# Both turns of a pair of 64 column heads ahead of values and scores in one step

## The reference

```
s = jnp.einsum('bhqd,bhld->bhql', qi, ko) * scale     # scores, masked
p = jax.nn.softmax(s, axis=-1)
o = jnp.einsum('bhql,bhld->bhqd', p, vo)              # 256 x 256 by 256 x 64 a head
y = (merge(o) * jax.nn.silu(g)) @ w_out
```

## Time and profile before

| | us |
|---|---|
| median of 3 runs | 780.57 (780.35 to 781.04) |
| profiled execution | 780.67 |
| its span, from the first to the last instruction | 778.9 |
| TensorE matmul busy | 762.0 |
| VectorE busy | 513.8 |
| ScalarE busy | 416.0 |
| GpSimd busy | 98.3 |
| granted TensorE clock, mean | 0.998 |

### The profile page before, as it was taken

One profiled execution on the slowest core, in us unless ns is written; L12 is line 12 of the kernel. 1 busy time (PEld: TensorE's weight loads), 2 busy tenths in 40 slices (PEclk: granted clock), 3 DMA queues, 4 the chain that ended last, 5 costly groups with the idle time before them and its releaser, 6 DMA issues.

```text
span 778.9 us, 12960 instructions
## 1 busy us (share of the span) xinstructions
PE 762.0 (98%) x5014; PEld 670.3 (86%) x5014; DVE 513.8 (66%) x816; ACT 416.0 (53%) x623; POOL 98.3 (13%) x74
## 2 busy tenths in 40 slices
PE   8999999999999999999999899999999999999997
PEld 7998877799978887999787699889777999999996
DVE  6985556666664558477866875787856755555554
ACT  5544445453664553446675567576655544444443
POOL 3341000000100004111300207700000000000002
PEclk9999999999999999999999999999999999999999
DMA  9965643344664544676833554765317575656541
GB/s 334 332 203 177 215 163 108 122 157 121 210 224 160 172 157 160 195 227 197 247 114 104 166 176 151 219 205 173 109 55 219 192 237 191 207 177 211 169 156 55
DMA packets 77659, 139.54 MB, mean 179 GB/s; under 512 B 7184, under 2 KB 15648, under 8 KB 77600
## 3 DMA queue, kind: packets, MB, share of 16 engines
q1 hardware_dynamic: 75744, 132.15, 52.4%
q0 software_dynamic: 1856, 6.57, 2.6%
HBM read 134.90 MB, written 1.06 MB: 175 GB/s over the span
## 4 chain that ended last, share of the span: by engine, by line
PE 87%; DVE 6%; issue 3%; POOL 2%; ACT 1%; DMA 1%; SPq 0%; POOLq 0%; ACTq 0%; DVEq 0%
PE acc L1081 13%; PE acc L1083 13%; PE acc L1082 13%; PE acc L1089 12%; PE acc L1091 12%; PE acc L1090 12%; DVE w_lo L810 2%; PE acc L1369 1%; PE acc L1403 1%; DMA raw<-in_w_in_even 1%; PE acc L1342 1%; PE acc L1282 1%; PE acc L1238 1%; PE acc L1353 1%; POOL b_lo L810 1%
## 5 line engine op out<-in xcount | busy, mean ns | idle before, releaser
L810 DVE TENSOR_TENSOR w_lo<-raw,w_hi 128x1024 fp32r<-128x1024 f32 (+1 forms) x224 | 275.3, 1245 | 171.3 <-ACT w_hi L790 90.2
L1089 PE MATMUL acc<-x_hi,w_hi 128*128 128x256 f32 x840 | 234.8, 280 | 1.5 <-DVE w_lo L810 1.1
L1091 PE MATMUL acc<-x_hi,w_lo 128*128 128x256 f32 x840 | 232.1, 276 | 0.0
L1090 PE MATMUL acc<-x_lo,w_hi 128*128 128x256 f32 x840 | 232.1, 276 | 0.0
L790 ACT ACTIVATE w_hi<-raw 128x1024 fp32r<-128x1024 f32 (+1 forms) x128 | 133.6, 1045 | 126.4 <-PE acc L1091 63.9
L780 ACT ACTIVATE w_hi<-raw 128x1024 fp32r<-128x1024 f32 x109 | 116.1, 1065 | 107.6 <-PE acc L1091 55.5
L1089 PEld LDWEIGHTS acc<-x_hi,w_hi 128*128 128x128 f32 x840 | 157.7, 188 | 4.1 <-issue 2.8
L1090 PEld LDWEIGHTS acc<-x_lo,w_hi 128*128 128x128 f32 x840 | 157.8, 188 | 0.8 <-issue 0.5
L1091 PEld LDWEIGHTS acc<-x_hi,w_lo 128*128 128x128 f32 x840 | 157.7, 188 | 0.0
L1081 PE MATMUL acc<-w_hi,cat_hi 128*128 128x512 f32 x272 | 108.9, 400 | 0.2 <-DVE w_lo L810 0.2
L1083 PE MATMUL acc<-w_hi,cat_lo 128*128 128x512 f32 x272 | 106.2, 390 | 0.0
(11 more groups left out here) (297 smaller groups left out, 903.0 us busy)
## 6 DMA issues: line engine op xcount, KB each, us to landing
raw<-in_w_ff SPq DMA_DIRECT2D x32, 1024.0 KB, 5.3
raw<-in_w_in_even SPq DMA_DIRECT2D x28, 1024.0 KB, 5.0
raw<-in_w_in_odd SPq DMA_DIRECT2D x16, 1024.0 KB, 5.4
raw<-in_w_in SPq DMA_DIRECT2D x16, 1024.0 KB, 5.6
raw<-in_w_out_even SPq DMA_DIRECT2D x12, 1024.0 KB, 5.4
raw<-in_w_out SPq DMA_DIRECT2D x4, 1024.0 KB, 5.3
raw<-in_w_in_even SPq DMA_DIRECT2D x4, 512.0 KB, 6.2
raw<-in_w_ukv_even SPq DMA_DIRECT2D x8, 256.0 KB, 3.2
```

Of the source, the lines that this page charges most:

```text
L810: ins = eng.tensor_tensor(lo, r, hi.bitcast(F32), ALU.subtract)
L1089: pe.matmul(o, wh[k][:, fs], hi[:, ka, :], start=start and f % 2 == 0, stop=False, skip_group_check=True)
L1090: pe.matmul(o, wh[k][:, fs], lo[:, ka, :], start=False, stop=False, skip_group_check=True)
L1091: ins = pe.matmul(o, wl[k][:, fs], hi[:, ka, :], start=False, stop=stop, skip_group_check=True)
```

## The change

The turns of the 64 column heads move. Both turns of a pair stand at the head of step n = (even head) + 4, then the values, if any are due, and then the scores. The first turn of a pair writes bank 1, columns 0 to 383, as before; the second writes the end of bank 1 (columns 384 to 511) and the first half of bank 2. The values use the second half of bank 2 alone. Waits: the second turn waits on TensorE for `out_read` of the unit before, or of the one before that while a pair of values is pending (`PENDING`); ScalarE makes both copies after both turns, the second after the values too; VectorE's gate waits for the copies.

```
+PENDING = {first + m: 1 if m > 1 and m + LAG < count else 0 for first, count in ((8, 16), (24, 8)) for m in range(1, count, 2)}
...
         for n in range(count + LAG + 2):
+            done = None
             if per_unit == 2:
+                if n % 2 == 0 and 0 <= n - LAG - 1 < count:
+                    step("turn", first + n - LAG - 1)
+                    step("turn", first + n - LAG)
                 for m in range(1, count, 2):
                     if n == values_at(m):
                         step("values", first + m)
+                        done = m
+            if n < count:
+                step("scores", first + n)
+            steps.extend(after)
+            after = []
+            if done is not None:
+                step("gate", UNIT[first + done])
+                if done == count - 1:
+                    step("low", UNIT[first + done])
-            if 0 <= n - LAG < count:
+            if per_unit == 1 and 0 <= n - LAG < count:
                 step("turn", first + n - LAG)
...
                 elif kind == "turn":            # TensorE
                     pe.wait_ge(*due("probs_ready", a + 1))
-                    if a:
+                    if a and (a < MLA_HEADS or a % 2 == 0):
                         pe.wait_ge(*due("turned_copied", a))
-                    for o0, c0 in ((0, 0), (P, P), (2 * P, 2 * P)):
-                        ins = pe.transpose(aux[:, 1, o0:o0 + P], pr[:, c0:c0 + P], ident)
+                    if a >= MLA_HEADS and a % 2:
+                        pe.wait_ge(*due("out_read", UNIT[a] - PENDING[a]))
+                        to = ((1, 3 * P), (2, 0), (2, P))
+                    else:
+                        to = ((1, 0), (1, P), (1, 2 * P))
+                    for c, (bank, o0) in enumerate(to):
+                        ins = pe.transpose(aux[:, bank, o0:o0 + P], pr[:, c * P:(c + 1) * P], ident)
...
-                            o = aux[64 * h:64 * h + 64, 2, (u % 2) * S + t * P:(u % 2 + 1) * S]
+                            o = aux[64 * h:64 * h + 64, 2, S + t * P:2 * S]
...
                 elif kind == "turn":            # ScalarE
-                    act.wait_ge(*due("probs_turned", a + 1))
-                    if a >= TURNED:
+                    paired = a >= MLA_HEADS
+                    act.wait_ge(*due("probs_turned", a + 2 if paired and a % 2 == 0 else a + 1))
+                    if paired and a % 2:
+                        act.wait_ge(*due("values_ready", a - 1))
+                    elif a >= TURNED:
                         act.wait_ge(*due("values_ready", a - TURNED + 1))
-                    own(act.activation(turned[:, a % TURNED, :], aux[:, 1, 0:3 * P], ACT.Copy), "turned_copied")
+                    o0 = 3 * P if paired and a % 2 else 0
+                    own(act.activation(turned[:, a % TURNED, :], aux[:, 1:3, :].rearrange("p b n -> p (b n)")[:, o0:o0 + 3 * P], ACT.Copy),
+                        "turned_copied")
...
-                    o = aux[:, 2, (u % 2) * S:(u % 2 + 1) * S]    # VectorE, gate
+                    if u >= MLA_HEADS:
+                        last = LAST_OF_UNIT[u]
+                        later = 2 if last + LAG + 2 < 24 or 24 <= last < 24 + BAND_HEADS - LAG - 2 else 0
+                        dve.wait_ge(*due("turned_copied", last + 1 + later))
+                        o = aux[:, 2, S:2 * S]
+                    else:
+                        o = aux[:, 2, (u % 2) * S:(u % 2 + 1) * S]
```

More of the change, by code:

```diff
@@ L263, in pipeline @@
         for n in range(count + LAG + 2):
+            done = None
+            if per_unit == 2:
+                if n % 2 == 0 and 0 <= n - LAG - 1 < count:
+                    step("turn", first + n - LAG - 1)
+                    step("turn", first + n - LAG)
+                for m in range(1, count, 2):
+                    if n == values_at(m):
+                        step("values", first + m)
+                        done = m
             if n < count:
```

## The result

| | before | after |
|---|---|---|
| median, us | 781.01 (780.35 to 781.46, 7 runs) | 783.06 (782.59 to 783.88, 7 runs) |
| profiled execution, us | 780.67 | 782.84 |
| its span, us | 778.9 | 781.0 |

After over before is 1.003, with a 95% interval of 1.0019 to 1.0042: the kernel is slower by 2.05 us. 780.9 was forecast, with a range of 779.2 to 782.5; 783.06 lies above it. The changed lines shift the numbers: TensorE's turn is L1381, values L1415, scores L1360; on VectorE the weight split `w_lo` is L817, the maximum L2114 and L2115, the normalise L2124 to L2127.

A forecast was written before the change was run, and what follows sets the result against it. TensorE, busy 762.0 of 778.9 us, was taken as the bound. Terms +0.3 - 0.78 - 0.16 + 0.78 + 0.15 = +0.29 on 780.67 gave 780.96, or 780.9 us as median; range 779.2 to 782.5.

The forecast's parts named there:

- Streaming: On TensorE, two turns, values and scores joined cost 2.53 us against 2.48 for the old groups; +0.3 us taken overall.
- Waits that go: A turn's wait for ScalarE's copy at step 5 goes (-0.78 us), and the values' wait at step 15 (-0.16).
- Tails: In each pipeline's last pair, the values wait for both turns and two ScalarE copies: +0.39 us each, +0.78 together.
- New waits (a) to (c): Second turn on `out_read` (0, at most 0.5 us), VectorE's gate on turn copies (0), ScalarE's second copy on values (0).
- `out_read` rival: TensorE stands at the second turn in four places when VectorE's gate is late: some +0.5 us, 781.4; chance 0.08.
- Side effect (d): VectorE's weight split comes ahead of the scores' maximum at even steps, delaying step 8's scores: +0.15 us, bounds 0 and 1.5.
- VectorE becomes late before step 8: Rival: VectorE loses another 2 us between steps 4 and 7 and TensorE stands at the scores: 782.9 us; chance 0.15.

The follow-up runs named there:

- copy_first: The kernel before, with only ScalarE's copy of an odd head's turn moved ahead of the exponentials of the same even step: 780.25 us, 0.9987 of before.
- hold_restored: The changed kernel, with VectorE's weight split again held behind the next scores where turn or values steps now stand between: 780.39 us, 0.9995 of before.

## Why the prediction was wrong, step by step

**Streaming: right.** T T V S is 2.51 us, predicted 2.53, against 2.48 for S V T and T apart. The unknown entry from T to V is 383.21 - 382.46 - 0.66 = 0.09 us, the same as from a main to S. The Trainium skill, TensorEngine Tiling (Array Packing), section Key Properties, says that a change of tiling mode drains TensorE. The trace agrees: there are as many changes of mode as before, and the time is the same within 0.03. In sum streaming is nearer 0 than the +0.3 taken: with the hold restored the first pipeline differs by -0.62, of which the two waits that go and the one tail are -0.78 - 0.16 + 0.39 = -0.55, and the band by +0.40, its tail +0.39.

**Waits that go: right.** The 0.8 us is in no list after, and V of step 15 starts 413.52 - 413.20 = 0.32 after the last main, where it was 0.48. copy_first takes them by the same cause and gains 0.92; the sum was 0.94.

**Tails: right.** V of the last pair starts 1.78 after T T; predicted 1.07 + 0.33 + 0.39 = 1.79. The two stages give 0.45 and 0.39 back with single turns.

**New waits (a) to (c): right at nothing.** TensorE never stands inside T T (six transposes in 0.66), which ends the `out_read` rival, and in VectorE's waits no gate waits for a copy.

**Side effect (d): the step that failed.** It named the mechanism, the place and the margin (1.0 in hand, S wanted at about 384.0: it was 384.01), and took +0.15 where the lost holds cost 1.67 + 1.05 = 2.72. Four errors:

- It wrote that the splits "have a piece and a half in hand" and asked only when a split is needed. It did not ask what the split covered (the wait for the exponentials), nor when the split can start. This is why "takes up about half", said of the idle 1.44 us at 376.81, did not come true. In the rows of before the `w_hi` for that split is finished only at 377.08, behind the idle time; after, the split waited 1.11 for it, since ScalarE too was late, and the next normalise 0.72 for exponentials. Moving a split ahead of the maximum delayed the next maxima by its whole length, 1.17.
- It overlooked two places. The `rest` of step 14 and of band step 6 lose their hold through `values`, and the second alone is 1.04, the whole price in the band. Term (d) had nothing for the band.
- It priced a split at 1.22, though the 2.24 us row had been cited as what may happen, and that row too lies beside a product of GpSimd (last section). Delayed, the split met the next one: 2.57, worth about 1.0.
- Its bounds, 0 to 1.5, were missed narrowly in the first pipeline (1.67), and no bound was set for the band.

The sum with the measured terms: the change with the hold kept is -0.62 + 0.40 = -0.22, with the 2.72 of the lost hold on top +2.50; the spans differ by 2.1, the rest lying in the varying stretch between. The rival "VectorE becomes late before step 8" was the case that happened, with its place and its point of decision (the maximum of head 15 ends past 384.0: it ended at 385.4). That its time, 782.9, is so near 783.06 is in part luck: it priced 2 us at this one place, where 1.67 were lost, and did not name the band, which brought 1.05. It had a chance of 0.15, on the ground that "the like must hit once more, at the new place". It need not be chance. GpSimd's product ends at 377.83 in the trace of before, and the split moved ahead cannot start before 377.08, so a meeting could be read off.

Left open: no run separates the 0.39 that VectorE lost in idle time between the maxima of heads 13 and 15 from the rest.

## What to carry to other kernels

Before moving a step in a written order, look for every rule that reads "the next step": such a rule changes its answer without a line of it being edited, and each place where it does is a term of its own. A piece of work that is not urgent may still be the filler of a latency (here one of 1.06 us between a maximum and its normalise); ask what it covers, not only when it is due. And first ask for the smallest edit with the same effect: here a reordered copy on ScalarE gave 0.92 us in the first pipeline, where moving all turns gave 0.62 with the hold kept, and cost 1.05 without it.

## What the runs showed of the hardware

The fp32 split of VectorE (128x1024, two inputs in SBUF, 1.22 us alone) grows by nearly the time that it overlaps with GpSimd's product: 1.35 for an overlap of 1.50 (after), 0.19 for 0.33 (hold_restored: 377.53 to the product's end at 377.86), 0.32 for 0.46 (before: 377.37 to 377.83). The Trainium skill, SBUF — State Buffer, section "SBUF: two separate sides", says that the port pair which the two engines share is an exclusive lock, which such a VectorE operation and a reading GpSimd operation take for a whole instruction each. The trace agrees with a block rather than a shared rate: the split that came second grew by 1.35, while the product that came first took 2.40 us, against 2.36 before. Four quarter products in place of one cut the loss from 1.35 to 0.39, while GpSimd's own time grew from 2.40 to 3.82. Two engines that take turns would do that, but the three further starts are in it too, and the four products were not timed alone. The maximum at 376.81, which reads the scores from PSUM, shows no such loss beside the same product: 0.29 us, as elsewhere.

The scaling of 128 columns that took 2.24 us at 362.10, 0.29 elsewhere, lies beside such a product too. GpSimd's timeline of the kernel before:

```profile
361.74 2.52 POOL L2415 TENSOR_TENSOR R<-R,trig 128x1024 f32<-128x1024 f32 x1 [21.75 <-ACT R L1606]
```

They overlap from 362.10 to 364.26, 2.16 us, and the scaling loses 1.95. No run moved this pair apart.

A stop of TensorE costs more than its bracket: 0.77 us of idle was 1.05 of the band, and 1.56 was 1.67 of the first pipeline. The scores of step 8 start 385.64 - 383.21 = 2.43 behind the values in the changed kernel and 0.80 with the hold restored, so they are 1.63 late, 0.07 more than the bracket says.
